# FFN input product of a decoder layer: eighteen weight units as seven block products instead of eight

## The reference

```
h = rmsnorm(x, norm_ffn)                       # x: 512 x 1024
gt, up = split(h @ w_ffn_in)                   # w_ffn_in: 1024 x 5632
x = x + (silu(gt) * up) @ w_ffn_out            # w_ffn_out: 2816 x 1024
out = rmsnorm(x, norm_final)
```

## Time and profile before

| | us |
|---|---|
| median of 3 runs | 799.15 |
| profiled execution, own time | 799.31 |
| its span | 797.5 |
| PE busy / DVE busy / ACT busy / POOL busy | 789.9 / 406.2 / 290.0 / 24.8 |
| granted TensorE clock, mean | 0.999 |

### The profile page before, as it was taken

The page is one execution under the profiler, slowest core; times in us unless marked ns, Lnnn a source line. Parts: engine busy times, 40 slices in busy tenths (PEclk is TensorE's granted clock), DMA queues, the critical chain, the costliest instruction groups (busy, mean ns, idle before and its releaser), DMA issues.

```text
span 797.5 us, 11178 instructions
## 1 busy us (share of the span) xinstructions
PE 789.9 (99%) x4382; PEld 659.1 (83%) x4382; DVE 406.2 (51%) x816; ACT 290.0 (36%) x524; POOL 24.8 (3%) x36
## 2 busy tenths in 40 slices
PE   9999999999999999999999999999999999999996
PEld 7878899889878787888889888888888888888885
DVE  5935333556766776656518533444433444422347
ACT  6112155243647666643317221222221223222235
POOL 1301000000000000003100000000000000000000
PEclk9999999999999999999999999999999999999999
DMA  7931354330311111164231333322333321222202
GB/s 236 345 116 53 106 102 137 83 110 4 106 53 54 54 55 41 40 185 133 105 106 54 106 105 105 102 77 84 105 105 105 102 87 75 106 105 105 105 1 106
DMA packets 100216, 79.08 MB, mean 99 GB/s; under 512 B 16929, under 2 KB 94801, under 8 KB 100177
## 3 DMA queue, kind: packets, MB, share of 16 engines
q1 hardware_dynamic: 99936, 78.26, 32.9%
q10 hardware_dynamic: 240, 0.29, 0.1%
HBM read 75.34 MB, written 3.19 MB: 98 GB/s over the span
## 4 chain that ended last, share of the span: by engine, by line
PE 99%; DMA 0%; ACT 0%; DVE 0%; issue 0%; ACTq 0%; DVEq 0%
PE bank L1451 28%; PE bank L1452 28%; PE bank L1453 28%; PE bank L1684 2%; PE bank L1703 2%; PE bank L1671 2%; PE bank L1585 1%; PE bank L1626 1%; PE bank L1607 1%; PE bank L1548 1%; PE bank L1475 1%; PE bank L1492 1%; PE bank L1698 1%; PE bank L1498 0%; PE bank L1501 0%; PE bank L1638 0%
## 5 line engine op out<-in xcount | busy, mean ns | idle before, releaser
L1451 PE MATMUL bank<-h_hi,w_hi 128*128 128x512 f32 (+1 forms) x368 | 140.0, 380 | 0.0
L1452 PE MATMUL bank<-h_lo,w_hi 128*128 128x512 f32 (+1 forms) x368 | 139.8, 380 | 0.0
L1453 PE MATMUL bank<-h_hi,w_lo 128*128 128x512 f32 (+1 forms) x368 | 139.8, 380 | 0.0
L1451 PE MATMUL bank<-n_hi,w_hi 128*128 128x512 f32 x272 | 108.8, 400 | 0.0
L1453 PE MATMUL bank<-n_hi,w_lo 128*128 128x512 f32 x272 | 106.1, 390 | 0.0
L1452 PE MATMUL bank<-n_lo,w_hi 128*128 128x512 f32 x272 | 106.0, 390 | 0.0
L889 DVE TENSOR_TENSOR w_lo<-w_raw,w_hi 128x2048 fp32r<-128x2048 f32 (+2 forms) x29 | 64.5, 2224 | 79.6 <-ACT w_hi L596 79.5
L1451 PEld LDWEIGHTS bank<-h_hi,w_hi 128*128 128x128 f32 x368 | 69.2, 188 | 13.1
L1453 PEld LDWEIGHTS bank<-h_hi,w_lo 128*128 128x128 f32 x368 | 69.2, 188 | 13.1
L1452 PEld LDWEIGHTS bank<-h_lo,w_hi 128*128 128x128 f32 x368 | 69.2, 188 | 12.9
L809 ACT ACTIVATE tanh_g<-gate_scaled 128x512 f32<-128x512 f32 x22 | 13.9, 632 | 180.4 <-DVE gate_scaled L1336 180.4
(11 more groups left out here) (222 smaller groups left out, 1162.6 us busy)
## 6 DMA issues: line engine op xcount, KB each, us to landing
w_raw<-in_w_ffn_in_dram SPq DMA_DIRECT2D x44, 512.0 KB, 4.6
w_raw<-in_w_in_dram SPq DMA_DIRECT2D x37, 512.0 KB, 4.8
w_raw<-in_w_ffn_out_dram SPq DMA_DIRECT2D x22, 512.0 KB, 3.8
w_raw<-in_w_out_dram SPq DMA_DIRECT2D x8, 512.0 KB, 3.7
w_raw<-in_w_in_dram SPq DMA_DIRECT2D x12, 256.0 KB, 4.5
xs<-in_x_dram SPq DMA_DIRECT2D x4, 512.0 KB, 5.0
wck_k<-in_w_ck_dram SPq DMA_DIRECT2D x1, 2048.0 KB, 11.8
wck_v<-in_w_cv_dram SPq DMA_DIRECT2D x1, 2048.0 KB, 14.7
```

The costliest lines, as they stand in the source:

```text
L1451: pe.matmul(dst, w[0], x_[0], start=start, stop=False)
L1452: pe.matmul(dst, w[0], x_[1], start=False, stop=False)
L1453: return pe.matmul(dst, w[1], x_[0], start=False, stop=stop)
```

## The change

Units 3 to 20 (18 of the 22; index n = 0 to 17) are computed with Strassen's scheme in Winograd's form. The 1024 input rows are cut in two, the 256 columns of a unit (gate, up) in two, and the 512 tokens in two. Instead of eight products of (512 rows x 128 columns) by (512 rows x 256 tokens), seven are made, each of 4 chunks x 3 = 12 matmuls of 256 columns. What is summed, and where:

- Once, ahead of unit 3: four token-side sums `t7`. GpSimd makes three of them with seven tensor_tensor of 128x1024 elements (the first waits for the last `h_lo`), VectorE the fourth with three tensor_tensor of 128x1024, put between the inverse square root and the read of `spread_r`. ScalarE and VectorE split the four (four casts, four subtractions of 128x1024). `t_hi` lies where `x2` was, so `x2` (2 MB) is stored to DRAM and later loaded back, by one DMA each on SyncE's queue.
- For each unit: four weight sums on GpSimd (tensor_tensor of 128x512, `weight_sums`); the cast and the subtraction of the unsummed blocks, 1024 and 512 elements (`plain_hi`, `plain_lo`), and of the four sums, 2048 (`sums_hi`, `sums_lo`).
- For each unit, after the products: one copy of a product on ScalarE (`keep_m1`, 256 elements), seven VectorE additions of 256 elements that read a bank (`up_to_u2`, `up_to_u3`, `three_blocks` with four, `last_block`), the scaling of the gate on GpSimd (`scaled_gate`, 512), tanh on ScalarE, and two VectorE multiplications (`seven_act`, 512 each, now from SBUF alone).

A unit uses four banks, and units alternate between banks 4 to 7 and 0 to 3. TensorE waits before product 2 for the summed weights, before product 6 for `up_to_u3`, and before product 7 for the second addition of `three_blocks`. On VectorE the order of one unit is: `last_block` of the unit before, `plain_lo` of the next unit, `up_to_u2`, `seven_act` of the unit before, `up_to_u3`, `sums_lo` of the next unit, `three_blocks`. On GpSimd, once unit n has ended: the last weight sum of unit n+2 (it overwrites what unit n's product 7 read), `scaled_gate` of unit n, then, from product 3 of unit n+1 on, the first three weight sums of unit n+3. On ScalarE the cast of unit n+2's sums stands behind the tanh of unit n. The output product takes token tiles 0 and 1 ahead of 2 and 3 in its first unit.

```diff
+            pool.wait_ge(h_lo, 2 * TT)
+            link(pool.tensor_tensor(t_f[:, 2], h_f[:, second, late], h_f[:, first, late], ALU.subtract))
+            link(pool.tensor_tensor(t_f[:, 2], t_f[:, 2], l_f[:, second, late], ALU.add))
+            pool.tensor_tensor(t_f[:, 2], t_f[:, 2], l_f[:, first, late], ALU.subtract).then_inc(t_made, 1)
...
+            def weight_sums(i, j, begins=False):
+                s = 1 - j
+                pool.wait_ge(raw_full[s], i * 32 + raw_count(U_IN + SEVEN_FROM + j))
...
+                    pool.wait_ge(m_done, i * 14 + (7 * j - 11))
+                pool.tensor_tensor(to[:, 2], w[:, 0:4, 0:P], w[:, 0:4, P:256], ALU.subtract).then_inc(s_sums, 1)
...
+                    pool.wait_ge(m_done, i * 14 + (7 * j - 7))
+                pool.wait_ge(s_sums, i * 8 + (4 * j + 3))
+                pool.tensor_tensor(to[:, 3], w[:, 4:8, 0:P], to[:, 1], ALU.subtract).then_inc(s_sums, 1)
+            def scaled_gate(i, j):
+                pool.wait_ge(u_sums, i * 14 + (7 * j + 7))
+                pool.tensor_tensor(gs[:, 1 - j, :], gs[:, 1 - j, :], rrow[:], ALU.mult).then_inc(sg_ready, 1)
...
+            with pool.Fori(1, SEVEN_N // 2 - 1) as i:
+                scaled_gate(i - 1, 1)
+                weight_sums(i + 1, 0)
+                scaled_gate(i, 0)
+                weight_sums(i + 1, 1)
...
+            with dve.Fori(1, SEVEN_N // 2 - 1) as i:
+                last_block(i - 1, 1)
+                plain_lo(i, 1)
+                up_to_u2(i, 0)
+                seven_act(i - 1, 1)
+                up_to_u3(i, 0)
+                sums_lo(i, 1)
+                three_blocks(i, 0)
+                last_block(i, 0)
...
+                a = 4 * s
+                pe.wait_ge(wa_lo, i * 4 + (2 * j + 2))
+                pe.wait_ge(gu_free, i * 2 + (j + 4))
+                product(a, 0, plain(0, 4), turned(0, early))
+                pe.wait_ge(hi_done, i * 2 + (U_IN + SEVEN_FROM + j + 1))
+                pe.wait_ge(lo_done, i * 2 + (U_IN + SEVEN_FROM + j + 1))
+                product(a + 1, 0, summed(1), mixed(1))
+                product(a + 2, 0, summed(2), mixed(2))
+                product(a + 3, 0, summed(0), mixed(0))
+                pe.wait_ge(m1_out, i * 2 + (j + 1))
+                product(a, 256, plain(4, 8), turned(4, early))
+                pe.wait_ge(u_sums, i * 14 + (7 * j + 2))
+                product(a + 2, 256, [v[s][1][:] for v in (ahi7, alo7)], mixed(3))
+                pe.wait_ge(u_sums, i * 14 + (7 * j + 4))
+                product(a + 3, 256, summed(3), turned(4, late))
```

More of the change, by code:

```diff
@@ L519, in _, with load_out @@
                     load_in(s, i * 2 + s, i * 2 + (U_IN + s - 1))
[L520 to L526 removed]
+            def load_out(i, s):
+                sp_.wait_ge(lo_done, i * 2 + (U_OUT + s - 1))
+                dst = slot_view(raw, s, 2, D)
+                for k in range(2):
+                    sp_.dma_start(dst[:, k, :], w_ffn_out[0, bass.ds((i * 2 + s) * 256 + P * k, P), :]
+                                  ).then_inc(raw_full[s], 16)
+            with sp_.Fori(0, 1) as i:
+                for s in range(2):
+                    load_out(i, s)
+            sp_.wait_ge(x2_out, 16)
+            sp_.wait_ge(m_done, 7 * SEVEN_N)
+            sp_.dma_start(x2[:], x2_rows).then_inc(x2_back, 16)
+            with sp_.Fori(1, FT // 4) as i:
+                for s in range(2):
+                    load_out(i, s)
             load(N_UNITS - 1)
@@ L589, in _ @@
+            scaled_gate(SEVEN_N // 2 - 2, 1)
+            scaled_gate(SEVEN_N // 2 - 1, 0)
+            scaled_gate(SEVEN_N // 2 - 1, 1)
         @block.scalar
@@ L815, in _ @@
             ffn_in(0, 1)
+            parts_of_t()
+            plain_hi(0, 0, True)
             tanh_gate(0, 1)
[L817 to L825, removed]
+            sums_hi(0, 0, True)
+            plain_hi(0, 1, True)
+            tanh_gate(1, 0)
+            keep_m1(0, 0, True)
+            sums_hi(0, 1, True)
+            plain_hi(1, 0)
+            keep_m1(0, 1)
+            seven_tanh(0, 0)
+            sums_hi(1, 0)
+            with act.Fori(1, SEVEN_N // 2 - 1) as i:
+                plain_hi(i, 1)
+                keep_m1(i, 0)
+                seven_tanh(i - 1, 1)
+                sums_hi(i, 1)
+                plain_hi(i + 1, 0)
+                keep_m1(i, 1)
+                seven_tanh(i, 0)
+                sums_hi(i + 1, 0)
+            i = SEVEN_N // 2 - 1
+            plain_hi(i, 1)
+            keep_m1(i, 0)
+            seven_tanh(i - 1, 1)
+            sums_hi(i, 1)
+            act.wait_ge(raw_full[1], raw_count(U_OUT - 1))
+            act.wait_ge(m_done, 7 * SEVEN_N - 7)
+            act.copy(whi[1][:, 0:2048], raw[1][:, 0:2048]).then_inc(hi_done, 1)
+            keep_m1(i, 1)
+            seven_tanh(i, 0)
+            act.wait_ge(raw_full[0], raw_count(U_OUT))
+            act.wait_ge(m_done, 7 * SEVEN_N)
+            act.copy(whi[0][:, 0:2048], raw[0][:, 0:2048]).then_inc(hi_done, 1)
+            seven_tanh(i, 1)
+            act.copy(ahi[:, 0, :, :], actt[:, 0:2, :]).then_inc(a_hi, 1)
+            act.wait_ge(g_scaled, 4)
+            act.activation(tg[:, 1, :], gs[:, 1, :], ACT.Tanh, scale=0.5).then_inc(gu_tanh, 1)
             act.wait_ge(gu_free, 24)
@@ new lines, in sums_lo, with up_to_u2 @@
+            def sums_lo(i, j):
+                s = 1 - j
+                dve.wait_ge(hi_done, i * 2 + (U_IN + SEVEN_FROM + j + 1))
+                dve.tensor_tensor(slo7[s], s7[s][:], shi7[s].bitcast(F32), ALU.subtract).then_inc(lo_done, 1)
+            def up_to_u2(i, j):
+                dve.wait_ge(m1_out, i * 2 + (j + 1))
+                dve.wait_ge(m_done, i * 14 + (7 * j + 2))
+                dve.tensor_tensor(u2s[:], ps[4 * (1 - j) + 1][:, 0:256], m1s[:], ALU.add).then_inc(u_sums, 1)
@@ new lines, in last_block, with seven_act @@
+            def last_block(i, j):
+                s = 1 - j
+                dve.wait_ge(u_sums, i * 14 + (7 * j + 4))
+                dve.wait_ge(m_done, i * 14 + (7 * j + 7))
+                dve.tensor_tensor(gs[:, s, 256:512], ps[4 * s + 3][:, 256:512], u4s[:], ALU.add).then_inc(u_sums, 1)
+            def seven_act(i, j):
+                s = 1 - j
+                dve.wait_ge(sg_tanh, i * 2 + (j + 1))
+                dve.scalar_tensor_tensor(out=tm[:, 0, :], in0=tg[:, s, :], scalar=1.0, in1=gs[:, s, :],
+                                         op0=ALU.add, op1=ALU.mult).then_inc(sg_mul, 1)
+                dve.wait_ge(sg_mul, i * 2 + (j + 1))
+                tile_ = actt[:, i * 2 + (j + SEVEN_FROM), :]
+                dve.tensor_tensor(tile_, tile_, tm[:, 0, :], ALU.mult).then_inc(gu_free, 1)
@@ L1351, in _ @@
             ffn_in_lo(0, 1)
+            parts_of_t(0)
+            parts_of_t(1)
             ffn_in_act(0, 1)
[L1353 to L1363, removed]
+            plain_lo(0, 0)
@@ new lines, in _ @@
+            sums_lo(0, 0)
+            ffn_in_act(1, 0)
+            plain_lo(0, 1)
+            up_to_u2(0, 0)
+            up_to_u3(0, 0)
+            sums_lo(0, 1)
+            three_blocks(0, 0)
+            last_block(0, 0)
+            plain_lo(1, 0)
+            up_to_u2(0, 1)
+            seven_act(0, 0)
+            up_to_u3(0, 1)
+            sums_lo(1, 0)
+            three_blocks(0, 1)
+            with dve.Fori(1, SEVEN_N // 2 - 1) as i:
[7 more added lines that the diff above has]
+                last_block(i, 0)
+                plain_lo(i + 1, 0)
+                up_to_u2(i, 1)
+                seven_act(i, 0)
+                up_to_u3(i, 1)
+                sums_lo(i + 1, 0)
+                three_blocks(i, 1)
@@ new lines, in _ @@
+            i = SEVEN_N // 2 - 1
+            last_block(i - 1, 1)
+            plain_lo(i, 1)
+            up_to_u2(i, 0)
+            seven_act(i - 1, 1)
+            up_to_u3(i, 0)
+            sums_lo(i, 1)
+            three_blocks(i, 0)
+            last_block(i, 0)
+            up_to_u2(i, 1)
+            seven_act(i, 0)
+            up_to_u3(i, 1)
+            ffn_in_lo(FT // 2 - 1, 0)
+            three_blocks(i, 1)
+            last_block(i, 1)
+            ffn_in_lo(FT // 2 - 1, 1)
+            seven_act(i, 1)
@@ L1838, in _, with seven, product, plain @@
             ffn_first()
[L1839 to L1842, removed]
+            def seven(i, j):
+                s = 1 - j
+                early, late = slice(0, 256), slice(256, 512)
+                def product(bank, c, w, x_):
+                    for k in range(4):
+                        ins = split_product(ps[bank][:, c:c + 256], [v[:, k, :] for v in w], [v[:, k, :] for v in x_],
+                                            k == 0, k == 3)
+                    ins.then_inc(m_done, 1)
+                def plain(lo, hi):
+                    return [v[s][0][:, lo:hi, :] for v in (ahi7, alo7)]
+                def summed(b):
+                    return [v[s][:, b] for v in (shi7, slo7)]
+                def turned(lo, tokens):
```

(12 more changed lines are left out.)

136 lines of the change are left out of this document (132 added, 4 removed).

## The result

The changed kernel takes 859.83 us (median of 4 runs, 859.12 to 861.20) against 799.11 for the kernel before (4 runs): a ratio of 1.0756 (95% interval 1.0734 to 1.0778), 60.7 us slower. Forecast was 841 in 805 to 864. The profiled execution is the slowest of the four runs, 861.20; its FFN begins 1.7 us later than before (the last `h_lo` at 436.00 against 434.30).

A forecast was written before the change was run, and what follows sets the result against it. TensorE was taken to bound the kernel, with 99% of the chain. Opening +14.4, first unit +4.8, fifteen units +23.6 and the last -0.8 made +42.0 on 799.31: 841.3, taken as 841; range 805 to 864.

The forecast's parts named there:

- What binds, and what will bind: Units 3 to 20: TensorE holds 99% of the chain; after the change, gaps ahead of product 7, released by VectorE's `three_blocks`.
- What is removed: Each seven-product unit: 84 matmuls, 10.08 us in place of 10.88, saving 0.80 us, 14.4 over 18 units.
- The exclusion: VectorE instructions with two SBUF inputs and GpSimd instructions reading SBUF exclude each other; together 10.6 us a unit.
- The walk through one unit: Loop unit followed instruction by instruction: 12.45 us, of it 3.6 stood still on VectorE; TensorE idles 2.4.
- one more sum ahead each time: Loop rival: one further GpSimd sum gets in first, 13.7 us a unit, 860 us in total; chance 20%.
- main case: Loop units at 12.45 us, without a further GpSimd sum getting in first; 841 us in total; chance 50%.
- The opening: Ahead of unit 3: GpSimd's token sums delay VectorE and TensorE; unit 3 starts at 478.4 against 464.0, +14.4 us.
- If the stand at the spread goes, most of this returns as later waits for the same VectorE queue: Opening: without TensorE's 8.5 us stand at `spread_r`, most of the loss remains; bound of the part +10 us.
- The first unit: First seven-product unit: unit 4's weight sums start only when unit 2 has ended; it takes 15.7 us, +4.8.
- Storing `x2` and loading it back at no cost: DMA: the store takes 9 to 18 us, ends ahead of the casts; the way back hides under unit 21; nothing added.

The follow-up runs named there:

- b1: Against the kernel before: seven products only in every second unit from 5 to 19, all sums and the gate on VectorE; 793.01 us, ratio 0.9917.
- e2: Against the changed kernel: GpSimd's five loop instructions a unit read only two elements, a memset writes the rest; 795.79 us.

## Why the prediction was right, and where it was off

Point by point, in the order of its steps.

- What binds, and what will bind: right. In the loop TensorE waits for VectorE's `three_blocks` and `up_to_u3`, 44.7 us in all, and but for 0.4 us in the first unit for nothing else.
- What is removed: right, and a little small. At full clock 256-wide matmuls start 0.12 us apart; a unit of seven products without waits takes 9.95 to 9.98 (b1, e2) where 10.08 was forecast.
- The exclusion: right in kind, and shown by two runs from opposite sides: nearly all of GpSimd's reads taken away at the same order (795.8), and GpSimd's work given to VectorE (814.2). Instructions with two SBUF inputs stand to the end of GpSimd's; the seven bank additions, 18 times each, take 0.40 to 0.43 without exception.
- The walk through one unit: mis-sized, 12.45 against 13.62, and this is where most of the missing 19 us lie (15.5, below). Of the four stands the walk had 0.8, 1.1, 1.0, 0.75; measured were 0.94, 1.09, 0.97, 0.74. The fifth, 1.04 at the first multiplication, it had put aside as the rival "one more sum ahead each time, 13.7 a unit: 860". That rival, given 20%, is what happened in the steady unit, 13.62. Its total of 860 against 859.83 is closer than it deserves: its opening was 3.0 too short and its units together about as much too long. The main case failed in the order of two requests 0.1 us apart, which a walk from rounded rows can't settle; the range held because its upper part was set by this rival. The run with the additional wait turned the order round and came to 838.95. That this is near the main case's 841 is partly luck too: the opening was again 3.0 longer than forecast, and the units were 5 us shorter, since in every second one the second multiplication passed as well.
- The opening: +14.4 forecast, +17.4 measured (unit 3 starts at 483.1, less the 1.7, against 464.0). The total is near, but its terms are not (times here less the 1.7):
  - The row factor was ready 1.8 us later than worked out (455.7 against 453.9), since two of the three tensor_scalar stood for 2.2 to 2.4 us each: the walk took only two-input instructions as exposed.
  - The price of a stand left out the clock: after the spread the 512-wide matmuls start 0.43 us apart instead of 0.23, and unit 1 ends at 465.5, where 461.7 was forecast.
  - Ahead of unit 2 TensorE was to stand 5.5 us and stood 0.5. The forecast had put a weight sum in front of the low part of unit 2's weights; that sum waits for the end of unit 1 and started 2.1 us after the low part, which took its own 2.29.
  - Ahead of unit 3 it was to stand 0.3 and stood 4.3. The same weight sums met the four `t_lo` instead (9.01 us for the four, 4.62 in e2).
  - The first matmuls of unit 3 are 0.215 us apart, at the lower clock.
- "If the stand at the spread goes, most of this returns as later waits for the same VectorE queue": right in the prediction, and then forgotten in the expectation for the run that tried it, which forecast 850 to 853, a gain of 7 to 10 us; it was 2.
- The first unit: 15.7 forecast, 12.8 measured, but the second took 14.5; together 27.3 against 28.15.
- Storing `x2` and loading it back at no cost: nothing waited for either; the store landed in 7.9 us.

The sum over units 3 to 20 was +27.6 forecast and +43.1 measured (from unit 3's first matmul to the output product's first, 483.10 to 733.19 against 464.02 to 670.97); with the opening's 3.0 that is 18.5 of the 18.8 us by which the forecast was short.

## What to carry to other kernels

Before work is given to GpSimd, add up what VectorE's instructions with two SBUF inputs and GpSimd's reads need exclusively, not what each engine is busy: here both engines were below TensorE's time and together above it (10.6 by the forecast's estimate against 10 us of matmuls). Here GpSimd's help cost more than it brought, even against a VectorE that then became full (859.8 against 814.2). Only two orders of the shared work were tried, the changed kernel's and the one with the additional wait (12.1 a unit); whether some order comes near the 10.6 is open. Where a change gives each unit a little and each unit's helper work doesn't fit, put it in every second unit, and spread its preparation over the units ahead. And where a walk has two requests within a tenth of a microsecond, price both orders and give them equal chances.

## What the runs showed of the hardware that was not expected

- A one-input tensor_scalar on VectorE, 4 elements, f32 as well as int32, stands behind both kinds of GpSimd instruction that it met here: 2.36 and 2.23 us beside a 1024-element sum, 0.96 and 0.93 beside a memset of 0.95 that only writes. Two-input instructions stand behind the sum, not behind the memset. The Trainium skill has both halves (SBUF — State Buffer, "Who interferes with whom": a VectorE instruction in a 2-port mode, which tensor_scalar can enter, contends with GpSimd; one with two SBUF inputs contends with a GpSimd instruction that reads SBUF, not with one that only writes it); the trace agrees, by these rows, even at 4 elements. Whether these instructions did run in such a mode no run here shows.
- Of the twelve 4-element instructions of the inverse square root exactly two get done for each GpSimd sum: the one that stood until the sum's end, and one more before the next sum begins (the sums are linked by semaphore). Six of the twelve stood.
- GpSimd stands in the same way, even for two elements: in e2 its tensor_tensor of 128x2, at 0.19 when alone, took 1.54 beside VectorE's subtraction of 2048 elements.
- TensorE's granted clock fell from 1.00 to 0.55 and 0.50 in the 5 us stretches in which it stood for 10.2 us at the spread, and to 0.62 and 0.70 around the 4.3 us wait ahead of unit 3. In the loop, with waits of up to 2 us in each 13.6, it stood at 1.00 from 500 to 550 and at 0.97 in each 50 us from there to 700: three short spells at the lower level (577 to 580, 631.5 to 634.5 and 672.5 to 675.5 show 0.50), with TensorE busy all through them.
